# Gated stages with one product of 512 columns for a block's high part

## What is computed

```python
def conv_ffn(x, w_up, conv_w, w_down):
    h = causal_dwconv(x @ w_up, conv_w)      # 1024 -> 5632, 3 taps along the rows
    g, v = jnp.split(h, 2, axis=-1)          # 2816 each
    return (jax.nn.silu(g) * v) @ w_down     # 2816 -> 1024
```

## Time and profile before

| | |
|---|---|
| median of 3 runs | 1420.31 us (1419.86 to 1421.29) |
| the profiled execution | 1418.98 us |
| its span | 1417.4 us |
| granted TensorE clock, mean | 0.986 of full |
| TensorE busy | 1376.4 us |
| VectorE busy | 963.2 us |
| ScalarE busy | 725.1 us |
| GpSimd busy | 172.4 us |
| read from HBM | 236.27 MB, 169 GB/s |

### The profile page before, as it was taken

How to read it: one execution, slowest core, us unless ns; L and a number is a source line. 1 busy time by engine, 2 the same in 40 slices (tenths; PEclk the granted TensorE clock), 3 DMA queues, 4 the chain that set the end, 5 groups by cost and what they waited for, 6 DMA issues and landing times.

```text
span 1417.4 us, 23108 instructions
## 1 busy us (share of the span) xinstructions
PE 1376.4 (97%) x9591; PEld 1243.4 (88%) x9591; DVE 963.2 (68%) x1526; ACT 725.1 (51%) x1063; POOL 172.4 (12%) x142
## 2 busy tenths in 40 slices
PE   7999999999999999999988999999999999899998
PEld 6887899999888899997976799999689998799997
DVE  4876476667785866667787566556557997665565
ACT  4654364455442554553655464445456875544443
POOL 3570300000000000000034100000222214000000
PEclk8999999999999999999999999999999999899999
DMA  7622175555462555552542055555344445355541
GB/s 273 220 103 119 63 264 178 224 184 179 176 251 96 182 205 208 182 191 103 209 149 89 30 213 197 214 184 180 139 181 154 145 150 184 129 195 201 195 181 60
DMA packets 36697, 240.39 MB, mean 170 GB/s; under 512 B 3889, under 2 KB 6257, under 8 KB 9202
## 3 DMA queue, kind: packets, MB, share of 16 engines
q1 hardware_dynamic: 36594, 238.92, 46.7%
HBM read 236.27 MB, written 2.64 MB: 169 GB/s over the span
## 4 chain that ended last, share of the span: by engine, by line
PE 89%; DVE 6%; ACT 2%; issue 1%; DMA 1%; POOL 0%; SPq 0%; DVEq 0%; ACTq 0%
PE ps L404 23%; PE ps L366 18%; PE ps L368 17%; PE ps L367 17%; PE ps L542 2%; PE ps L537 2%; PE ps L1702 1%; PE ps L864 1%; DVE wlo L317 1%; PE ps L1729 1%; PE ps L515 1%; DVE ar L905 1%; PE ps L2002 1%; PE ps L1599 1%; PE ps L1082 1%
## 5 line engine op out<-in xcount | busy, mean ns | idle before, releaser
L366 PE MATMUL ps<-XS,whi 128*128 128x256 f32 x2088 | 598.6, 287 | 3.5 <-DVE wlo L311 2.9
L367 PE MATMUL ps<-XS,whi 128*128 128x256 f32 x2088 | 593.7, 284 | 0.0
L368 PE MATMUL ps<-XS,wlo 128*128 128x256 f32 x2088 | 593.7, 284 | 0.0
L317 DVE TENSOR_TENSOR wlo<-raw,whi 128x2048 fp32r<-128x2048 f32 (+1 forms) x178 | 398.7, 2242 | 108.0 <-ACT whi L294 107.9
L294 ACT ACTIVATE whi<-raw 128x2048 fp32r<-128x2048 f32 x203 | 386.9, 1907 | 119.8 <-PE ps L404 70.5
L366 PEld LDWEIGHTS ps<-XS,whi 128*128 128x128 f32 x2088 | 403.8, 193 | 9.1 <-issue 4.1
L367 PEld LDWEIGHTS ps<-XS,whi 128*128 128x128 f32 x2088 | 403.9, 193 | 2.0 <-issue 0.4
L368 PEld LDWEIGHTS ps<-XS,wlo 128*128 128x128 f32 x2088 | 403.6, 193 | 0.0
L404 PE MATMUL ps<-whi,MS 128*128 128x512 f32 x960 | 273.4, 391 | 0.0
L404 PEld LDWEIGHTS ps<-whi,MS 128*128 128x128 f32 x960 | 177.6, 188 | 35.2 <-issue 0.4
L302 POOL TENSOR_TENSOR wlo<-raw,whi 128x512 fp32r<-128x512 f32 x114 | 155.5, 1396 | 310.7 <-ACT whi L294 222.7
(11 more groups left out here) (290 smaller groups left out, 1360.4 us busy)
## 6 DMA issues: line engine op xcount, KB each, us to landing
raw<-in_up SPq DMA_DIRECT2D x88, 1024.0 KB, 4.8
raw<-in_down SPq DMA_DIRECT2D x44, 1024.0 KB, 4.8
raw<-in_hg_t SPq DMA_DIRECT2D x16, 1024.0 KB, 4.8
raw<-in_od_t SPq DMA_DIRECT2D x8, 1024.0 KB, 4.9
raw<-in_ev_a SPq DMA_DIRECT2D x6, 1024.0 KB, 9.8
raw<-in_wa_o SPq DMA_DIRECT2D x6, 1024.0 KB, 4.8
raw<-in_hg_o SPq DMA_DIRECT2D x6, 1024.0 KB, 4.7
raw<-in_ev_o SPq DMA_DIRECT2D x4, 1024.0 KB, 6.2
```

The costliest lines, as they stand in the source:

```text
L317: ve.tensor_tensor(lo[:, c], r[:, c], hi[:, c].bitcast(F32), ALU.subtract).then_inc(w_lo_v)
L366: pe.matmul(d, hi[:, c], S[:, k, 0:256], start=(k == 0), stop=False)
L367: pe.matmul(d, hi[:, c], S[:, k, 256:512], start=False, stop=False)
L368: last = pe.matmul(d, lo[:, c], S[:, k, 0:256], start=False, stop=(k == 7))
```

## The change

In the gated stages `project_wide` takes the place of `project`. A block's high part is multiplied with all 512 columns of `XS`, high and low parts of the rows at once, into a whole bank; the low part with the 256 high columns goes on top of the bank's first half. Each up tile so fills two banks, and the two halves of a bank have still to be added: ScalarE copies the second half into a new buffer `fS`, VectorE adds the first half onto it (`added_dve`). Scales and taps then read `fS`. The gate, the product with the value and the chunk's parts of tile j-1 move behind the copies and sums of tile j. TensorE waits before tile j for the sum of tile j-2. The down tiles come one pair later, and the chunks go round in 8 places of `MS` in place of 6; the order becomes up 0 to 5, down 0, up 6, 7, down 1, and so on to up 20, 21, down 8, 9, 10. Nothing outside the gated stages changes.

`silu_act`, `mixed_act`, `taps_dve` and `product_dve` hold the instructions of before under new names: the gate, `ms_high(j % 8, ...)`, the taps (reading `fS`, after a wait for the sum), and the product with the value.

```diff
def schedule():
         for m in range(11):
             s.extend((up, layer * 22 + j, 2048, 1) for j in (2 * m, 2 * m + 1))
-            if 0 < m < 9:
-                s.append((down, layer * 11 + m - 1, 2048, 1))
-        s.extend((down, layer * 11 + m, 2048, (1, 0, 4)[m - 8]) for m in (8, 9, 10))
+            if m > 1:
+                s.append((down, layer * 11 + m - 2, 2048, 1))
+        s.extend((down, layer * 11 + m, 2048, (0, 4)[m - 9]) for m in (9, 10))
...
+        def project_wide(m, banks, ready=None):
+            hi, lo = weights(m)
+            for i in range(2):
+                d = banks[i]
+                for k in range(8):
+                    if ready and i == 0:
+                        ready(k)
+                    c = slice(1024 * i + 128 * k, 1024 * i + 128 * k + 128)
+                    pe.matmul(d[:, 0:512], hi[:, c], XS[:, k, 0:512], start=(k == 0), stop=False)
+                    last = pe.matmul(d[:, 0:256], lo[:, c], XS[:, k, 0:256], start=False, stop=(k == 7))
+            last.then_inc(w_done)
...
+        fS = [R(512) for _ in range(3)]
+        f_cb, f_sm = mark("f_cb"), mark("f_sm")
...
         def ffn_pe(k):
-                    if j == 2:
+                    if j == 1:
                         filled(n)
-                    if j >= 4:
-                        pe.wait_ge((f_cv if k < 2 else f_mu).sem, 22 * k + j - 3)
-                    project(ffn_up(k, j), bank[4 + j % 4], xs_both(n) if j == 0 else None)
+                    if j >= 2:
+                        pe.wait_ge(f_sm.sem, 22 * k + j - 1)
+                    project_wide(ffn_up(k, j), bank[4 + 2 * (j % 2):6 + 2 * (j % 2)], xs_both(n) if j == 0 else None)
-                if 0 < m < 9:
-                    d = m - 1
-                    accumulate([ffn_down(k, d)], MS, [2 * d % 6, (2 * d + 1) % 6], 1024, accs,
+                if m > 1:
+                    d = m - 2
+                    accumulate([ffn_down(k, d)], MS, [2 * d % 8, (2 * d + 1) % 8], 1024, accs,
...
         def ffn_act(k):
             for j in range(22):
                 t = ffn_up(k, j)
                 ac.wait_ge(w_done, DONE[t])
-                if j >= 4:
-                    ac.wait_ge(f_mu.sem, 22 * k + j - 3)
+                for i in range(2):
+                    b = bank[4 + 2 * (j % 2) + i]
+                    ac.activation(o[:, 256 * i:256 * i + 256], b[:, 256:512], ACT.Copy).then_inc(f_cb.up())
+                if j:
+                    silu_act(k, j - 1)
+                ac.wait_ge(f_sm.sem, 22 * k + j + 1)
...
+                if j:
+                    mixed_act(k, j - 1)
                 act_weights(t + 3)
-                ac.wait_ge(f_ga.sem, 22 * k + j + 1)
-                ac.activation(h, g[:, 0:256], ACT.Silu if k < 2 else ACT.Gelu_apprx_tanh).then_inc(f_si.up())
-                ac.wait_ge(f_mu.sem, 22 * k + j + 1)
-                ms_high(j % 6, h)
-                if j % 2 and 0 < j // 2 < 9:
+                if j % 2 and j > 4:
                     act_weights(t + 4)
+            silu_act(k, 21)
+            mixed_act(k, 21)
             act_weights(NEXT[2 * k + 1])
...
+        def added_dve(k, j):
+            o = fS[j % 3]
+            for i in range(2):
+                ve.wait_ge(f_cb.sem, 44 * k + 2 * j + i + 1)
+                c = slice(256 * i, 256 * i + 256)
+                ins = ve.tensor_tensor(o[:, c], bank[4 + 2 * (j % 2) + i][:, 0:256], o[:, c], ALU.add)
+            ins.then_inc(f_sm.up())
...
         def ffn_dve(k):
             for j in range(22):
+                added_dve(k, j)
+                if j:
+                    product_dve(k, j - 1)
+                taps_dve(k, j)
+                if j:
+                    ms_low((j - 1) % 8, fH[(j - 1) % 3])
                 dve_weights(t + 3)
-                ms_low(j % 6, h)
-                if j % 2 and 0 < j // 2 < 9:
+                if j % 2 and j > 4:
                     dve_weights(t + 4)
+            product_dve(k, 21)
+            ms_low(21 % 8, fH[21 % 3])
             dve_weights(NEXT[2 * k + 1] - (k == 1))
```

More of the change, by code:

```diff
@@ L101, in ffn_up @@
 def ffn_up(k, j):
-    return FIRST["ffn", k] + (j if j < 2 else 3 * (j // 2) - 1 + j % 2 if j < 20 else j + 8)
+    return FIRST["ffn", k] + (j if j < 4 else 3 * (j // 2) - 2 + j % 2)
 def ffn_down(k, d):
-    return FIRST["ffn", k] + (3 * d + 4 if d < 8 else 22 + d)
+    return FIRST["ffn", k] + (3 * d + 6 if d < 9 else 22 + d)
 LAST = [FIRST["ev_o"] + 3, ffn_down(0, 10), FIRST["od_o"] + 3, ffn_down(1, 10),
@@ L1316, in ffn_pe, with silu_act, mixed_act @@
                 for j in (2 * m, 2 * m + 1):
-                    if j == 2:
+                    if j == 1:
                         filled(n)
-                    if j >= 4:
-                        pe.wait_ge((f_cv if k < 2 else f_mu).sem, 22 * k + j - 3)
-                    project(ffn_up(k, j), bank[4 + j % 4], xs_both(n) if j == 0 else None)
-                if 0 < m < 9:
-                    d = m - 1
-                    accumulate([ffn_down(k, d)], MS, [2 * d % 6, (2 * d + 1) % 6], 1024, accs,
[L1325 to L1328, removed]
+                    if j >= 2:
[4 more added lines that the diff above has]
+                    accumulate([ffn_down(k, d)], MS, [2 * d % 8, (2 * d + 1) % 8], 1024, accs,
+                               lambda c, tt, d=d: ready(2 * d + 1, tt) if c == 2 * d % 8 else None, d == 0, False)
+            accumulate([ffn_down(k, 9), ffn_down(k, 10)], MS, [2, 3, 4, 5], 1024, accs,
+                       lambda c, tt: ready(16 + c, tt), False, True)
+        def silu_act(k, j):
+            ac.wait_ge(f_ga.sem, 22 * k + j + 1)
+            ac.activation(fH[j % 3], fG[j % 4][:, 0:256], ACT.Silu if k < 2 else ACT.Gelu_apprx_tanh).then_inc(f_si.up())
+        def mixed_act(k, j):
+            ac.wait_ge(f_mu.sem, 22 * k + j + 1)
+            ms_high(j % 8, fH[j % 3])
         def ffn_act(k):
@@ L1336, in ffn_act @@
                 t = ffn_up(k, j)
-                g, h, o = fG[j % 4], fH[j % 3], bank[4 + j % 4]
+                g, o = fG[j % 4], fS[j % 3]
                 w = taps(k, j)
                 ac.wait_ge(w_done, DONE[t])
-                if j >= 4:
-                    ac.wait_ge(f_mu.sem, 22 * k + j - 3)
+                for i in range(2):
[4 more added lines that the diff above has]
+                ac.wait_ge(f_sm.sem, 22 * k + j + 1)
                 if k < 2:
@@ L1355, in ffn_act, with taps_dve @@
                     act_weights(t + 4)
+            silu_act(k, 21)
+            mixed_act(k, 21)
             act_weights(NEXT[2 * k + 1])
+        def added_dve(k, j):
[5 more added lines that the diff above has]
+            ins.then_inc(f_sm.up())
+        def taps_dve(k, j):
+            g, o = fG[j % 4], fS[j % 3]
+            w = taps(k, j)
+            ve.wait_ge(f_sm.sem, 22 * k + j + 1)
+            ve.wait_ge(f_in.sem, 22 * k + j + 1)
+            if k < 2:
+                da, db = g[:, 0:256], g[:, 256:512]
+                oa, ob = o[:, 0:256], o[:, 256:512]
+                ve.scalar_tensor_tensor(da[:, 1:256], oa[:, 0:255], w[0][1], da[:, 1:256], ALU.mult, ALU.add).then_inc(dv.up())
+                ve.scalar_tensor_tensor(db[:, 1:256], ob[:, 0:255], w[1][1], db[:, 1:256], ALU.mult, ALU.add).then_inc(dv.up())
+                ve.wait_ge(dv.sem, dv.n - 1)
+                ve.scalar_tensor_tensor(da[:, 2:256], oa[:, 0:254], w[0][0], da[:, 2:256], ALU.mult, ALU.add).then_inc(f_ga.up())
+                ve.wait_ge(dv.sem, dv.n)
+                ve.scalar_tensor_tensor(db[:, 2:256], ob[:, 0:254], w[1][0], db[:, 2:256], ALU.mult, ALU.add).then_inc(f_cv.up())
+            else:
+                d = g[:, 0:256]
+                ve.scalar_tensor_tensor(d[:, 1:256], o[:, 0:255], w[0], d[:, 1:256], ALU.mult, ALU.add).then_inc(dv.up())
+                ve.wait_ge(dv.sem, dv.n)
+                ve.scalar_tensor_tensor(d[:, 0:255], o[:, 1:256], w[2], d[:, 0:255], ALU.mult, ALU.add).then_inc(f_ga.up())
@@ L1358, in ffn_dve, with product_dve @@
+        def product_dve(k, j):
+            h = fH[j % 3]
+            other = fG[j % 4][:, 256:512] if k < 2 else fS[j % 3][:, 256:512]
+            ve.wait_ge(f_si.sem, 22 * k + j + 1)
+            if k < 2:
+                ve.wait_ge(f_cv.sem, 22 * k + j + 1)
+            ve.tensor_tensor(h, h, other, ALU.mult).then_inc(f_mu.up())
         def ffn_dve(k):
```

23 lines of the change are left out of this document (removed).

## The result

| | before | changed |
|---|---|---|
| median | 1420.09 us (1417.52 to 1421.29, 4 runs) | 1412.01 us (1411.64 to 1412.58, 4 runs) |
| the profiled execution | 1418.98 us | 1411.72 us |
| its span | 1417.4 us | 1410.4 us |

The medians are 8.1 us or 0.57% apart. The ratio of the two kernels is 0.9947, 95% interval 0.9933 to 0.9962, so the change makes the kernel faster. The direction and the range were right; the size is a little under half of the 16.8 us that I forecast.

The account below looks back on a forecast made before the run. TensorE, busy 97% and 89% of the chain, was taken to bound the kernel. 1418.98 - 16.8 = 1402.2 for the profiled execution, plus 1.3 for the median gave 1403.5 us; range 1396 to 1414.

Parts of the forecast that it names:

- The price of the new step: TensorE, gated stages' up tiles: 347.8 ns a step in place of 359.7, 1408 steps, 16.8 us gained; bounds 6.6 and 28.
- rival (a): Up tiles: the price at a change of width stays, 355 ns a step, gain 6.6 us, time 1413.7; chance 0.12.
- the stage's start: Six up tiles in a row: VectorE loses 3.2 us against 4.6 us of lead; no stall, about 1.5 us left.
- My walk: One up tile followed through VectorE: about 6.1 us a step, above TensorE's 5.57, but a pair fits, 14.4 of 16.6 us.
- Copies and sums: 176 blocks: 67 us more for ScalarE, 74 us for VectorE, neither on the chain, hidden by slack.
- Banks by pairs: TensorE's head-of-tile wait: sum of tile j-2 ready 1.2 to 1.8 us after its tile, nearly 4 us to spare.
- Down tiles one pair later: Gated stages: products wait longer for ready chunks, the ring grows from 6 to 8 of 12, nothing overwritten early.
- The end of a stage: Last chunk ready 8.45 us after the last up tile, needed at 8.7; costed at nothing, 2 us kept for the range.
- (b): Up tiles: the merge is worth nothing because a matmul's price is its columns; time 1420, chance 0.05.
- The Trainium skill's rule: Merged matmuls: columns over 2.4 GHz plus 2.5 ns each, so a gain of 3.5 us and 1416.8; counted within (b).
- (c): Stage ends: last chunk and norm's start late by 1 to 2 us in each stage, 1407 to 1411 us; chance 0.06.
- (d): Up tiles: VectorE becomes the bound through hand-offs with ScalarE; at 7.7 us a tile 24 us slower, 1444; chance 0.07.

Follow-up runs that it names:

- grouped kernel: Changed kernel, but in each block the eight matmuls of 512 columns come first, then the eight of 256: 1405.82 us, ratio 0.9908 to the kernel before.
- narrow kernel: Changed kernel with the merge alone undone, three matmuls of 256 columns a step, staging kept: 1421.47 us, ratio 1.0018 to the kernel before.
- banks kernel: Changed kernel with a tile's two blocks in turn: 512 and 256 into the first bank, 512 and 256 into the second, then the next chunk: 1409.27 us.
- pairs kernel: Changed kernel with both blocks of a tile in step: per chunk two matmuls of 512, one to each bank, then two of 256: 1404.33 us, ratio 0.9896.
- mirror: Changed kernel with every second step turned round, so widths go 512, 256, 256, 512 in one bank: 1404.00 us (one run).
- low part first: Changed kernel with the low part's 256-column matmul ahead of the 512 in all steps but a block's first: 1407.47 us (one run).
- early kernel: Changed kernel with the down tiles back at their old places, the ring of eight chunks kept: 1420.45 us, ratio 1.0007 to the kernel before.

## Why the prediction was wrong in size

**The price of the new step** failed. I had 227.9 + 119.9 = 347.8 ns, "both ways to the middle agree"; it measured 352.8, the upper end of my bounds being 355. The gain of 16.8 us at 11.9 ns a step became 9.7 us at 6.9 (1408 x 6.9). That is rival (a), the seam price that stays, to which I gave 0.12: it had 235 + 120 = 355 ns and 6.6 us. The mistake in the reasoning: I summed the price of a 512 inside a run of 512s and of a 256 inside a run of 256s, and took as support one seam of each kind. The rows had more. In the earlier trace rows the first four 512s behind a 256 take 0.93 us and not 0.91, so the seam was not over after one matmul; whoever alternates lives in the seam. The seam's own sum of one each, 235 + 113, failed too: in the alternation the two widths average 236.7 and 116.7, for the early 256 at 113 is only one of three. The grouped kernel shows that the steady prices were sizes of runs, and that they come true as soon as there are runs.

**The rest of the 16.8.** The down tiles pay too, which I had at nothing: 5.50 in place of 5.47 for nearly all of the 32 that follow two alternating up tiles, 1.1 us. TensorE waited for low parts around up tile 7 of the first two stages and lost 0.4 us in each (0.8); the view shows less as idle, 0.26 and 0.17, because the matmul before a wait counts as busy 0.16 us past the usual distance to the next start. I had 1.5 us of slack left there. What was wrong was the stage's start: the low part of up tile 3 was ready 2.0 us ahead of its tile, not 4.6, and at 0.4 us a tile the lead was gone by up tile 7. The six fast tiles of the third stage give 0.6 us back. 9.7 - 1.1 - 0.8 + 0.6 = 8.4; the other 0.4 of the 8.8 is in the fourth stage, whose first steps run at the lower clock (granted 0.50), for 3.9 us before and 2.8 us after.

My walk gave 6.1 us for VectorE's step and 6.05 was measured, but that was partly luck. The parts that I named (4.6 + 0.70 + 0.45 + 0.76 - 0.45 + 0.3) add up to 6.4. The 0.3 of longer waiting for the scales did not come, the wait is 0.72, and it was not in my total either. Outside the stages the profiled execution lost 1.8 us of the 8.8 (span less stages: 669.1 before, 670.9 after). What lies there differs by more than that between kernels that change nothing there, so I give it no cause.

**Copies and sums** hidden: right. ScalarE's copy measured 378 ns and VectorE's sum 418, where I had 381 and 422; the narrow kernel, which keeps them, is 0.9 to 4.3 us above the kernel before.

**Banks by pairs:** the outcome was right, the reasoning was not. No wait for a sum ended an idle time of TensorE. But I had the sum 1.2 to 1.8 us behind its tile and nearly 4 us to spare; at the start of the first stage it comes 4.2 us behind tile 0 and later behind each of the next five, because VectorE makes a low part ahead of the first sum and then falls behind. Tile 3 ends at 198.05, its sum at 203.16, and TensorE needs it at 203.70 for tile 5: 0.5 us to spare.

```profile
202.41 0.75 DVE L1392 TENSOR_TENSOR ar<-ps,ar 128x256 f32<-128x256 f32 x2
```

In the banks kernel, whose tiles are shorter there, 0.05 us is left at this place, and tile 5 starts late by 0.13.

**Down tiles one pair later:** I costed the move at nothing and gave no price to its absence. Undone, it costs about 8 us.

**The end of a stage:** right, no wait. The last chunk was ready 8.24 us after the last up tile's end (344.23 to 352.47), 8.45 in my walk, 8.7 needed:

```profile
352.04 0.43 DVE L458 TENSOR_TENSOR MS<-ar,MS 128x256 fp32r<-128x256 f32 x1 [0.48 <-ACT MS L454]
353.85 2.29 DVE L317 TENSOR_TENSOR wlo<-raw,whi 128x2048 fp32r<-128x2048 f32 x1 [1.38 <-ACT whi L294]
356.06 0.68 DVE L614 SCALAR_TENSOR_TENSOR yb<-xn,ps 128x512 f32<-128x512 f32 x1
```

The norm behind the first stage began at 356.06, 11.8 us after the tile's end, 12.3 in my walk, and its later start was hidden: TensorE's second set of transposes starts 7.8 us after the stage's end in both kernels (361.90 to 369.70 before, 360.45 to 368.26 after).

**Rivals.** (a) is what happened. (b), that the merge is worth nothing: refuted, in the narrow kernel the same work unmerged is about 10 us slower. The Trainium skill's rule ("TensorE: Matmul & The Clock Gate", "Back-to-back issue gap": columns over 2.4 GHz plus 2.5 ns, which the section gives for the isolated gap of a single matmul) had 3.5 us for the merge; the trace disagrees, with 6.9 ns a merged matmul where the rule has 2.5, and the fastest step seen, 347 ns, is above the rule's 325. (c): no. (d), VectorE as the bound: right in its place, with a size of half a microsecond where it needed tens.

**A better version.** The pairs kernel beats both: 1404.33 us, 1.04% less than before (0.9896, 0.9880 to 0.9913). It has the same matmuls as the changed kernel (0.9947, 0.9933 to 0.9962) in another order. The mirror and the grouped kernel are level with it.

## What to carry to other kernels

A price read from a run of equal instructions holds in a run. If the change makes them alternate, look at what the rows show for several matmuls behind a change of shape, take that for the price, and try the order with half the changes or none: here it took another 7 us off (0.9947 to 0.9896), nearly as much as the change itself. When a product is made cheaper, walk the hand-offs of the engines behind it over the longest stretch without a rest, and move the work that gives them one.

## What the runs showed of the hardware

- Alternating matmuls of 512 and 256 float32r columns, each with its own weight load, settle in one of two repeating patterns: 347 ns a step (230 + 117, or 233 + 117 and 231 + 112 in turn) or 353.3 (236 + 113, 233 + 117, 241 + 120). The same code in the same kernel shows both; the pattern changed behind a down tile (third stage of the changed kernel), behind a start 0.13 us late (first stage of the banks kernel) and at an odd step (low part first). In the changed kernel 9 of the 88 up tiles run at 347: tiles 0 to 5 of the third stage, 6 of the first, 0 and 7 of the second. Of the 32 tiles that stand right behind a down tile, 31 run at 353. What sets the state stays open. That it is the standing of the weight load to the stream is theory P's picture; the runs show that the bank has no part in it and the order of widths has, not that the loads are the cause. The records of the loads hardly differ: a load starts 2 or 3 ns after the matmul that it runs beside in the pattern of 347 and 2 to 5 ns after it in that of 353, and it lasts 187 to 190 ns in both.
- At the lower clock level a 512 takes 427 ns and a 256 takes 213, the columns at 1.2 GHz and nothing more. The 13 ns beyond the columns that a matmul of either width pays at 2.4 GHz (227 and 120) are not there. From the changed kernel's fourth stage, just after a wait of TensorE, where the granted clock is 0.50 (1217.40 to 1219.00):

```profile
1217.41 0.76 PE L382 MATMUL ps<-XS,whi 128*128 128x512 f32 x1 [0.65 <-DVE XS L602]
1217.98 0.41 PE L383 MATMUL ps<-XS,wlo 128*128 128x256 f32 x1
1218.19 0.63 PE L382 MATMUL ps<-XS,whi 128*128 128x512 f32 x1
1218.62 0.41 PE L383 MATMUL ps<-XS,wlo 128*128 128x256 f32 x1
1218.83 0.63 PE L382 MATMUL ps<-XS,whi 128*128 128x512 f32 x1
```

- A wait of 2.1 us in the first stage of the early kernel was followed by the lower clock (granted 0.50 from 201.5 to 204.8, 1.00 from 204.9 on). The down tile behind it took 7.15 us. A wait of 2.0 us at the same place of the second stage was not followed by it, and the down tile there took 5.53, so the clock cost 1.6 us on top of the wait. What decides between the two is not shown.
